# Exchanging the rows of the rotation by transfers instead of a matmul, with a new order of the tail, column quarters in the router and an early exponential table

## What is computed

```python
def _apply_rope(x, cos, sin):                 # q and k of the differential heads, latent tokens
    xr, xc = jnp.split(x, 2, axis=-1)
    rot = jnp.concatenate([_rot_half(xr), _rot_half(xc)], axis=-1)   # (-x2, x1) in each half
    return x * cos + rot * sin
...
xs = _layer_norm(ALPHA * xs + g1 * a, ln1_g, ln1_b)                  # after the attention
h = xs * (1 + sc2) + sh2
aff = softmax(h @ w_router)                                          # 16 experts
g, idx = top_k(aff.T, cap)                                           # 64 latent and 16 context tokens each
y = (silu(h[idx] @ w_gate) * (h[idx] @ w_up)) @ w_down * g           # expert by expert, then added back
```

## Time and profile before

| | before |
|---|---|
| median of 3 runs | 1829.06 us (1828.54 to 1832.92) |
| profiled execution, its own time | 1828.47 us |
| its span, first to last instruction | 1826.7 us |
| TensorE busy | 1784.3 us, 98% |
| VectorE, ScalarE, GpSimd busy | 1105.3, 594.8, 102.2 us |
| mean granted TensorE clock | 0.992 of 2.4 GHz |

### The profile page before, as it was taken

How to read it: one execution, slowest core, us unless ns; L and a number is a source line. 1 busy time by engine, 2 the same in 40 slices (tenths; PEclk the granted TensorE clock), 3 DMA queues, 4 the chain that set the end, 5 groups by cost and what they waited for, 6 DMA issues and landing times.

```text
span 1826.7 us, 37594 instructions
## 1 busy us (share of the span) xinstructions
PE 1784.3 (98%) x15493; PEld 770.3 (42%) x15493; DVE 1105.3 (61%) x3398; ACT 594.8 (33%) x1276; POOL 102.2 (6%) x87
## 2 busy tenths in 40 slices
PE   8999989997999999999999999999999999999998
PEld 8999867763233333333333333333333333333333
DVE  3766866666747474655656474747464555647474
ACT  3222356552422223322323232222332232323233
POOL 0000122204000000000000000000000000000000
PEclk9999999997999999999999999999999999999999
DMA  9644331236999999999999999999999999999993
GB/s 382 255 168 167 125 123 58 65 144 271 404 409 424 408 425 408 425 406 425 410 426 407 417 417 410 425 410 425 410 425 411 426 411 425 411 417 412 417 411 139
DMA packets 103018, 637.19 MB, mean 349 GB/s; under 512 B 11600, under 2 KB 21840, under 8 KB 30144
## 3 DMA queue, kind: packets, MB, share of 16 engines
q1 hardware_dynamic: 97696, 618.19, 82.2%
q0 software_dynamic: 4864, 16.57, 3.3%
q10 hardware_dynamic: 288, 0.03, 0.0%
HBM read 620.09 MB, written 13.88 MB: 347 GB/s over the span
## 4 chain that ended last, share of the span: by engine, by line
PE 74%; ACT 1%; DVE 0%; issue 0%; DVEq 0%; ACTq 0%
PE ps L1700 49%; PE ps L1715 25%; ACT place L1813 0%; ACT place L1809 0%; ACT place L1816 0%; ACT place L1811 0%; DVE place L1891 0%; DVE place L1907 0%; PE ps L1744 0%; ACT place L1753 0%; DVE place L1888 0%; DVEq L1642 0%; ACT place L1806 0%; ACT place L1788 0%; ACT place L1785 0%
## 5 line engine op out<-in xcount | busy, mean ns | idle before, releaser
L1700 PE MATMUL ps<-place 128*32 128x512 f32 x4808 | 523.6, 594 | 0.5 <-ACT place L1753 0.5
L1843 DVE STREAM_TRANSPOSE place<-place 32x64 f32<-32x64 f32 x2112 | 495.1, 234 | 27.2
L1700 PE MATMUL ps<-ring,place 128*32 128x512 f32 x3528 | 384.0, 592 | 0.0
L1700 PEld LDWEIGHTS ps<-place 128*32 128x32 f32 x4808 | 156.4, 110 | 361.3 <-issue 359.7
L1830 DVE TENSOR_TENSOR place<-ps,place 96x512 f32<-96x512 f32 (+1 forms) x176 | 120.7, 686 | 251.5 <-ACT place L1763 245.3
L1715 PE MATMUL ps<-place 128*32 128x512 f32 x2424 | 263.7, 592 | 0.0
L1761 ACT ACTIVATE place<-ps 64x512 f32<-64x512 f32 x176 | 104.6, 594 | 484.3 <-PE ps L1700 484.2
L1700 PEld LDWEIGHTS ps<-ring,place 128*32 128x32 f32 x3528 | 114.7, 110 | 263.9 <-issue 263.4
L1715 PE MATMUL ps<-ring,place 128*32 128x512 f32 x1800 | 196.6, 592 | 0.0
L1860 DVE TENSOR_TENSOR place<-ps,place 64x512 f32<-64x512 f32 x15 | 10.2, 683 | 248.6 <-ACT place L1788 248.6
L1715 PEld LDWEIGHTS ps<-place 128*32 128x32 f32 x2424 | 78.8, 110 | 181.3 <-issue 181.3
(11 more groups left out here) (243 smaller groups left out, 1499.2 us busy)
## 6 DMA issues: line engine op xcount, KB each, us to landing
place<-in_w_exp SPq DMA_DIRECT2D x304, 1024.0 KB, 22.1
ring<-in_w_exp SPq DMA_DIRECT2D x224, 1024.0 KB, 22.0
ring<-in_w_late SPq DMA_DIRECT2D x16, 1024.0 KB, 11.2
ring<-in_w_in SPq DMA_DIRECT2D x12, 1024.0 KB, 6.6
ring<-in_w_ada SPq DMA_DIRECT2D x7, 1024.0 KB, 10.4
ring<-in_w_out SPq DMA_DIRECT2D x4, 1024.0 KB, 6.5
place<-in_near_bias SPq DMA_DIRECT2D x16, 256.0 KB, 3.5
ring<-in_xT SPq DMA_DIRECT2D x4, 640.0 KB, 9.0
```

Of the source, the lines that this page charges most:

```text
L1700: mm = eng.matmul((up_side(Q) if side else up_main(Q))[quad(q)], X[:, e % 2, half * HALF_K + k, quad(g)], w[:, k * 512:(k + 1) * 512], sta ...
L1843: ins = eng.transpose(hT[quad(q), b * FPC:(b + 1) * FPC, quad(g)], hid[quad(g), Q % 2, 2 * q * QUAD:2 * (q + 1) * QUAD])
```

## The change

The rotation matrix and its matmuls go. ScalarE issues 16 transfers in each group, each copying 16 rows of 2 KB from `qdf` or `kdf` to the exchanged place in a buffer `swapped` (in `h32`); the sign is put into the sine table. They stand between `leave(i, 3)` and `high(3 * i + 3)`. VectorE multiplies in SBUF.

```diff
-                    for n, src in enumerate((qdf, kdf)):
-                        eng.wait_ge(qk_copied, 4 * i + 3 + n)
...
-                        eng.matmul(ps[:, 6 + n, :], rotM, src[:, i, CTX:TOK], start=True, stop=True).then_inc(rot_ready, 1)
                     values(i, 1, high=False)
                     values(i, 2)
...
+                def swap_rows(i, n):
+                    src = (qdf, kdf)[n]
+                    eng.wait_ge(qk_copied, 4 * i + 3 + n)
+                    if i:
+                        eng.wait_ge(rope_done, 2 * (i - 1) + n + 1)
+                    for r in range(0, P, 32):
+                        eng.dma_start(swapped[r:r + 16, n, :], src[r + 16:r + 32, i, CTX:TOK]).then_inc(swapped_landed[n], 16)
+                        eng.dma_start(swapped[r + 16:r + 32, n, :], src[r:r + 16, i, CTX:TOK]).then_inc(swapped_landed[n], 16)
...
                     leave(i, 2)
                     leave(i, 3)
+                    if i == 0:
+                        eng.wait_ge(x_split, KT)
+                    for n in range(2):
+                        swap_rows(i, n)
                     if i + 1 < GROUPS:
                         high(3 * i + 3)
...
-                        eng.wait_ge(rot_ready, 2 * i + n + 1)
+                        eng.wait_ge(swapped_landed[n], 2 * P * (i + 1) // 2)
...
-                        eng.tensor_tensor(tmp, ps[:, 6 + n, :], sinT, ALU.mult).then_inc(rot_read, 1)
+                        eng.tensor_tensor(tmp, tmp, sinT, ALU.mult).then_inc(sin_applied, 1)
```

```diff
+                    bank = turn_bank(("quarters", s, 0))
                     for j in range(KT):
...
+                        q0 = j % 4 * 32
+                        mm = eng.matmul(ps[q0:q0 + E, bank, 0:P], wroute[:, j, :], h2T[:, j, :], start=(j < 4), stop=(j >= 4))
...
+                def sum_logits(s):
...
+                    eng.matmul(ps[:, bank, 0:E], quarters, fold, start=True, stop=True).then_inc(t_ready, 1)
```

A one-element exponential (`ready_exp`) follows the square roots at the steps and after the last `spread`, so that the table is loaded there:

```diff
                     if due("squares", k) is not None:
                         root(due("squares", k))
+                        ready_exp()
...
                     if due("moments", k) is not None:
                         spread(due("moments", k))
+                        ready_exp()
```

In the tail GpSimd's last two sums wait until all shares are read, and the fetch waits for the stores; one round of `first_half` moves ahead of `share_modulation(END)`, the logits of the last tile ahead of two index operations, and `merge` loses operations and signals the rows before the values:

```diff
-                eng.wait_ge(rest_modulated, 1)
+                eng.wait_ge(shares_read, TT)
                 start_sum(END - 1)
-                eng.wait_ge(shares_read, TT)
...
-                eng.wait_ge(rows_known, 1)
                 eng.wait_ge(rows_zero, 1)
-                fetch(eng, 0)
                 for b, n in enumerate((2, 2, 1)):
                     eng.wait_ge(acc_stored[b], 16 * n)
+                eng.wait_ge(rows_known, 1)
+                fetch(eng, 0)
...
+                first_half(range(5, 6))
                 share_modulation(END)
-                first_half(range(5, CAP_L // 8))
...
+                first_half(range(6, CAP_L // 8))
+                shift_logits(END)
+                keep_shares(END - 1)
+                share(END)
```

More of the change, by code:

```diff
@@ L227, in build @@
         v_copied = sem("v_copied")
-        rot_ready = sem("rot_ready")
-        rot_read = sem("rot_read")
+        swapped_landed = [sem(f"swapped_landed{n}") for n in range(2)]
+        sin_applied = sem("sin_applied")
         rope_done = sem("rope_done")
@@ L934, in build @@
         for k in range(GROUPS + 1, STEPS):
+            if due("route", k) is not None:
+                for name in ("quarters", "logits"):
+                    turn_no[name, due("route", k), 0] = len(turn_no)
             for n in range(len(TURNS)):
@@ L1030, in _ @@
                     if k == GROUPS + 4:
+                        for n in range(1, 4):
+                            eng.tensor_tensor(fold, fold if n > 1 else ident[:, 0:E], ident[:, 32 * n:32 * n + E], ALU.add).then_inc(fold_made, 1)
+                            eng.wait_ge(fold_made, n)
                         eng.wait_ge(ln_landed, 32)
@@ L1158, in turn_norm, with route @@
                         turn_tile("x", s, half, x1[:, s % 3, :])
-                def route(s, bank=O_BANK):
-                    if s >= END - 1:
-                        eng.wait_ge(logits_read, s)
-                    for j in range(KT):
[L1164 to L1171, removed]
+                def route(s):
+                    if s == END:
+                        eng.wait_ge(rest_modulated, 1)
+                    eng.wait_ge(t_copied, copies(("x", s, 1)))
+                    bank = turn_bank(("quarters", s, 0))
+                    for j in range(KT):
+                        q0 = j % 4 * 32
+                        mm = eng.matmul(ps[q0:q0 + E, bank, 0:P], wroute[:, j, :], h2T[:, j, :], start=(j < 4), stop=(j >= 4))
+                    mm.then_inc(t_ready, 1)
+                def sum_logits(s):
+                    eng.wait_ge(fold_made, 3)
+                    eng.wait_ge(t_copied, copies(("quarters", s, 0)))
+                    bank = turn_bank(("logits", s, 0))
+                    eng.matmul(ps[:, bank, 0:E], quarters, fold, start=True, stop=True).then_inc(t_ready, 1)
                 def turn_shares(s, bank=O_BANK):
@@ L1187, in _ @@
                         scores(eng, k)
+                    if due("route", k) is not None:
+                        sum_logits(due("route", k))
                     if k == GROUPS + 1:
@@ L1244, in _ @@
                 turn_norm(END)
-                route(END, bank=1)
+                route(END)
+                sum_logits(END)
                 turn_shares(END, bank=3)
@@ L1274, in root, with ready_exp @@
                     eng.activation(rms[:, 1, n], rms[:, 0, n], ACT.Sqrt).then_inc(rms_rt, 1)
+                def ready_exp():
+                    eng.activation(lam_s[:, 6:7], epsc, ACT.Exp)
                 def spread(s):
@@ L1292, in modulate, with keep_quarters, keep_logits @@
                         ins.then_inc(t_copied, 1)
+                def keep_quarters(s):
+                    use = turn_no["quarters", s, 0]
+                    if s:
+                        eng.wait_ge(t_ready, turn_no["logits", s - 1, 0] + 1)
+                    eng.wait_ge(t_ready, use + 1)
+                    eng.activation(quarters, ps[:, 4 + use % 2, 0:P], ACT.Copy).then_inc(t_copied, 1)
+                def keep_logits(s):
+                    use = turn_no["logits", s, 0]
+                    eng.wait_ge(t_ready, use + 1)
+                    eng.activation(aff[:, ORDER[s], :], ps[:, 4 + use % 2, 0:E], ACT.Copy).then_inc(t_copied, 1)
                 def raise_logits(s):
@@ L1505, in _ @@
                         maxima(eng, k)
+                    if due("route", k) is not None:
+                        shift_logits(due("route", k))
                     if k == GROUPS + 1:
@@ L1930, in constants @@
     j = np.arange(P)
[L1931 to L1936, removed]
     t = by_column(np.arange(LAT))
```

94 lines of the change are left out of this document (55 added, 39 removed).

## The result

| | before | after |
|---|---|---|
| median | 1828.8 us (4 runs) | 1854.24 us (4 runs, 1853.36 to 1855.41) |
| profiled execution, its span | 1828.47, 1826.7 us | 1853.46, 1851.7 us |
| TensorE, VectorE, ScalarE busy | 1784.3, 1105.3, 594.8 us | 1780.2, 1108.3, 600.6 us |
| mean granted clock | 0.992 | 0.984 |

The account below looks back on a forecast made before the run. TensorE's order was taken to set the first two stages, the experts to follow their start, only the tail being a chain over several engines. 9.1 + 3.6 + 5.1 - 1.5 - 1.3 - 2.4 = +12.6 gave 1841.1 us, range 1823 to 1852.

Parts of the forecast that it names:

- the price of an issue: ScalarE's queue, first stage: each of 16 transfers per group takes 0.475 us, 7.6 in all; ends 6.1 and 10.6.
- dear issues: Rival: issues cost 0.66 us each, as the SBUF-to-SBUF rows do; +24.5 us, 1853; chance 0.17.
- stalls of groups 0 to 2: First stage: TensorE waits 4.8 us for the value copy, each group 3.0 longer; +9.1 us, ends +4.5 and +18.
- clock after them: After each of three stalls TensorE runs 3.4 us at half speed, losing 1.7; +5.1 us, between 0 and 5.1.
- group 3, its clock with it: Context exponentials start at 208.7 in place of 205.05, so the next stage starts 3.6 us later (ends 2.1 and 6.6).
- router and early table in the attention: Attention: two router steps save 0.75 us each, -1.5; moving the table load into idle time saves 1.3.
- tail up to the fetch: Tail: the fetch goes at the last store's landing, 445.3, not at 447.79; -2.4 us, between 0 and -3.5.
- experts: Last stage: follows its start one for one, so what moves the fetch of the first rows moves the end.
- The landings: First stage: landings of the transfers cost nothing; if one took over 6 us, VectorE's weight split would be next late.
- The fast rival: Rival: issues don't hold ScalarE, so TensorE gains 6.9 us in the first stage; 12.1 less, 1816.4; chance 0.14.
- an activation between the issues: ScalarE, first stage: an activation starting between the issues would show the forecast wrong.

Follow-up runs that it names:

- matmul rotation: The changed kernel with its rotation given back to TensorE as two float32 matmuls in each group; 1825.57 us, ratio 0.9972 to the kernel before.
- GpSimd version: The changed kernel with its 64 transfers issued from GpSimd's queue in place of ScalarE's; 1817.59 us, ratio 0.9929 to the kernel before.
- transfers alone: The kernel before with only the rotation's exchange done by transfers from ScalarE's queue; 1862.83 us, ratio 1.0178 to the kernel before.
- GpSimd alone: The kernel before with only the rotation's exchange done by transfers, all 64 issued from GpSimd's queue; 1824.81 us, ratio 0.9962 to the kernel before.
- issues in gaps: The changed kernel with its 64 transfers moved into ScalarE's idle time, except the keys' eight of group 3; 1834.98 us, ratio 1.0028 to the kernel before.
- half the issues: The changed kernel with eight transfers of 32 rows per group, same bytes, halves not exchanged; 1826.99 us, ratio 0.9983 to the kernel before.
- source in HBM: The changed kernel with the 64 transfers reading the cosine table in HBM, rows not exchanged; 1845.16 us, ratio 1.0089 to the kernel before.

## Why the prediction was wrong

**The failed step** is the price of an issue: "I take 0.475, because those two have one plain run for each partition, as the new ones do". What counted was the source. The issues that read SBUF cost 0.61 with a start every 0.64 on this queue, those that read the table in HBM 0.44 with one every 0.47, at the same rows and bytes. The earlier trace rows held the right row, the only one whose two ends are both in SBUF, at 0.66; I set it aside for its three dimensions. The rival called dear issues, with its +24.5 and chance 0.17, is what happened. By the prediction's own working, 0.64 gives 16 x 0.64 = 10.2 in place of 7.6, which makes 5.6 in place of 3.0 for each of groups 0 to 2, and 6.2 for group 3: +23.0 with all other terms as they stood. The traces have 5.5 and 6.5 for these two. That +24.5 comes so close to the measured +25.0 is in part luck: its stalls, group 3 and clock are 2.3 too high in sum, and the attention, 3.1 too low, makes up for it.

**Term by term**, from the marks of the two profiled executions:

| term | predicted | measured |
|---|---|---|
| before the first stall | 0 | +0.3 |
| stalls of groups 0 to 2 | +9.1 | +16.5 (5.54 + 5.46 + 5.46) |
| clock after them | +5.1 | +4.1 (1.41 + 1.35 + 1.30) |
| group 3, its clock with it | +3.6 | +6.5 (20.9 to 27.4) |
| router and early table in the attention | -2.8 | +0.3 (27.4 to 27.7) |
| tail up to the fetch | -2.4 | -2.7 |
| experts | 0 | 0 |
| sum | +12.6 | +25.0 |

**The clock** after a stall was in the forecast at 1.7; it was about 1.35, since a part of the slow stretch lies within the stall.

**Router and table** were sized right. The savings are in the rows above, and the traced execution with the matmul rotation is 4.1 us shorter from the scores to the transpose, 1.5 of it from the lower clock at the first scores of before. In the changed kernel two stretches at the lower clock took them back. One follows a wait of 1.95 us at L1138, which before and the GpSimd version have as well. Only some executions lose the clock there; what decides is open.

**The tail** came as worked out: the fetch goes with the landing of the last store, 2.7 earlier (2.4 predicted). Against the two other traces with the old tail, transfers alone and GpSimd alone, which took 52.6 from the transpose to the fetch, it is 1.9 to 2.0.

**The landings** cost nothing in the changed kernel, as the prediction had it, since TensorE and VectorE were both held back by ScalarE. Once ScalarE is free they are the next limit, which the version with issues in gaps shows.

**The fast rival** (issues don't hold ScalarE) is refuted by half the issues and by their move to another queue. (The prediction took an activation between the issues as a sign for it. One does start there, at 67.87, but it is the last projection copy, which stands ahead of all issues in the program.) But what it promised for a free ScalarE, 12.1 less, came with GpSimd's queue. The Trainium skill ("DMA: Bandwidth & Descriptors", section "Issuing engines are not separate DMA queues") says that several issuing engines save only the sequencer's time, "usually small relative to the DMA itself". The first half agrees with these runs. The second doesn't fit transfers of 32 KB: an issue took 0.61 beside a median of 6.7 us to landing here, and 0.49 beside 1.8 on GpSimd's queue, and sixteen in a row, 0.64 apart, brought the whole loss.

## What to carry to other kernels

Cost a DMA issue as an instruction of the engine whose program it stands in. Take its price from a row with the same kind of source, destination and queue that stands in a series as yours will, and set the count times the price against the idle time at that very place, not against the engine's idle share. Before giving up such a change, look for an engine with nothing to do: the same 64 transfers, put into the kernel before alone, lost 1.8% on ScalarE's queue and gained 0.4% on GpSimd's. An issue in a gap is free only if the landing still comes before the reader's next work: here the keys' transfers, issued 1.1 us after the start of the keys' copies, held up nobody, and those issued 5.8 after it did.

## What the runs showed of the hardware that was not expected

- An issue of an SBUF-to-SBUF transfer of 32 KB costs 0.61 us on ScalarE's queue, start to start 0.64, and 0.49 on GpSimd's (means of the 64 issues there). The Trainium skill ("DMA: Bandwidth & Descriptors", section "Issuing engine by pattern") calls the hardware queues generally faster; for these issues GpSimd's was the cheaper one.
- With 32 rows of 2 KB in place of 16 the issue stayed at its price (seven in 4.62 us, 0.66 each).
- The first issue of a series is cheaper: on ScalarE's queue 0.51 to 0.52 against 0.61 in groups 1 to 3 of the changed kernel (0.60 in group 0), and 0.32 to 0.34 against 0.44 with the source in HBM. The 0.34 of the earlier trace rows is such a first one; the issue right behind it took 0.43. And right behind the eight SBUF-to-SBUF issues that begin at 230.18 in the trace of before, a load from HBM took 0.61 (L979), its twin after it 0.44 (L980). An issue may thus pay for the one ahead of it; no run tests that.
- In all four groups ScalarE's first issue starts 0.27 us before the last projection copy (67.60 against 67.87), though it stands behind it in the program.
- The same transfers land in very different times: a median of 6.7 us from ScalarE's queue in the changed kernel, in stretches with a transfer share of about 1; 2.2 in the gaps, 1.8 from GpSimd's, where half of them go in quiet time.
- TensorE's waits of 7.0 to 7.8 us at the value tile brought the clock to its lower level in all four groups. Those of 1.94 to 2.04 with half the issues left it at 1.00 in three groups and were followed by the lower level in the fourth. A wait of 1.95 in the attention was followed by the lower level in some executions and not in others. From the first scores to the 16x16 transpose, six kernels with the same work there (the change, matmul rotation, source in HBM, half the issues, gaps, GpSimd) took 166.8 to 170.9 us.
